# Hybrid attention/RWKV block: the norm behind the mixing reordered, weight roundings moved ahead, and the feed-forward loop's rounding turned by one unit

## The reference

```python
y = rwkv7_scan(rh, heads(decay), kh, vh, kk, ah)
mu = jnp.mean(y, axis=-1, keepdims=True)
var = jnp.mean(jnp.square(y - mu), axis=-1, keepdims=True)
y = ((y - mu) * lax.rsqrt(var + GN_EPS)).reshape(B, T, RW_WIDTH)
y = y * ln_gain.astype(f32) + ln_bias.astype(f32)
bonus = jnp.sum(rh * kh * r_k, axis=-1, keepdims=True) * vh
y = (y + bonus.reshape(B, T, RW_WIDTH)) * g          # o_rw
...
merged = (jax.nn.sigmoid(gate_sb) * (o_sb @ w_branch_sb[l])
          + jax.nn.sigmoid(gate_rw) * (o_rw @ w_branch_rw[l]))
h = h + rms_norm(merged @ w_out[l], norm_mix_post[l])
f = rms_norm(h, norm_ffn_pre[l])
f = (jax.nn.silu(f @ w_ffn_gate[l]) * (f @ w_ffn_up[l])) @ w_ffn_down[l]
h = h + rms_norm(f, norm_ffn_post[l])
```

## Time and profile before

| | us |
|---|---|
| runs (3) | 908.72, 908.95, 911.32; median 908.95 |
| profiled execution, its own time | 913.13 |
| its span, first to last instruction | 911.3 |
| TensorE busy (matmuls) | 878.2 (96% of the span) |
| VectorE / ScalarE / GpSimd busy | 483.1 / 412.6 / 88.8 |
| mean granted TensorE clock | 0.992 of 2.4 GHz |

### The profile page before, as it was taken

One profiled execution on the slowest core, in us unless ns is written; L12 is line 12 of the kernel. 1 busy time (PEld: TensorE's weight loads), 2 busy tenths in 40 slices (PEclk: granted clock), 3 DMA queues, 4 the chain that ended last, 5 costly groups with the idle time before them and its releaser, 6 DMA issues.

```text
span 911.3 us, 19043 instructions
## 1 busy us (share of the span) xinstructions
PE 878.2 (96%) x8257; PEld 728.0 (80%) x8257; DVE 483.1 (53%) x639; ACT 412.6 (45%) x576; POOL 88.8 (10%) x92
## 2 busy tenths in 40 slices
PE   4899999999999999999999999999999999999997
PEld 3899999877777778766787887888888888888886
DVE  5249998437767655636576654444444444422243
ACT  5246555449878765664453542333332222221231
POOL 1014434311010101022200000000000000000000
PEclk9899999999999999999999998999999999999999
DMA  9222322321101121141376413333333333233321
GB/s 286 82 74 67 93 82 81 125 62 38 48 27 38 38 71 39 37 128 50 91 226 203 147 47 93 92 92 92 92 92 92 92 92 93 92 115 93 93 93 69
DMA packets 109150, 83.34 MB, mean 91 GB/s; under 512 B 2910, under 2 KB 99464, under 8 KB 108824
## 3 DMA queue, kind: packets, MB, share of 16 engines
q1 hardware_dynamic: 109080, 82.29, 29.8%
HBM read 76.51 MB, written 5.77 MB: 90 GB/s over the span
## 4 chain that ended last, share of the span: by engine, by line
PE 87%; DVE 7%; ACT 3%; issue 2%; DMA 1%; SPq 0%; POOL 0%; POOLq 0%; DVEq 0%; ACTq 0%
PE psum L566 44%; PE psum L1784 17%; PE psum L1535 9%; PE psum L1572 6%; PE psum L1709 2%; DVE w_lo L556 2%; PE psum L1436 1%; PE psum L1719 1%; PE psum L1827 1%; PE psum L1690 1%; PE psum L1738 1%; DMA w_raw<-in_w_in 1%; DVE shift_diff L1121 1%; ACT w_hi L551 1%; DVE k_mod L1161 1%
## 5 line engine op out<-in xcount | busy, mean ns | idle before, releaser
L566 PE MATMUL psum<-h_hi,w_hi 128*128 128x512 f32 (+1 forms) x736 | 234.2, 354 | 7.5 <-DVE w_lo L556 5.8
L566 PE MATMUL psum<-h_lo,w_hi 128*128 128x512 f32 (+1 forms) x736 | 231.8, 351 | 0.0
L566 PE MATMUL psum<-h_hi,w_lo 128*128 128x512 f32 (+1 forms) x736 | 230.6, 349 | 0.0
L566 PEld LDWEIGHTS psum<-h_hi,w_hi 128*128 128x128 f32 x736 | 129.6, 191 | 30.2 <-DVE w_lo L556 7.0
L556 DVE TENSOR_TENSOR w_lo<-w_raw,w_hi 128x1024 fp32r<-128x1024 f32 x69 | 89.0, 1292 | 119.1 <-ACT w_hi L551 119.1
L566 PEld LDWEIGHTS psum<-h_lo,w_hi 128*128 128x128 f32 x736 | 129.5, 191 | 18.9 <-issue 1.0
L566 PEld LDWEIGHTS psum<-h_hi,w_lo 128*128 128x128 f32 x736 | 129.5, 191 | 18.1
L1382 DVE TENSOR_TENSOR w_lo<-w_raw,w_hi 128x1024 fp32r<-128x1024 f32 x44 | 53.8, 1225 | 135.1 <-ACT w_hi L1052 135.1
L551 ACT ACTIVATE w_hi<-w_raw 128x1024 fp32r<-128x1024 f32 x70 | 73.8, 1056 | 79.5 <-PE psum L1784 63.3
L1052 ACT ACTIVATE w_hi<-w_raw 128x1024 fp32r<-128x1024 f32 x44 | 46.3, 1055 | 69.8 <-PE psum L566 69.8
L1784 PE MATMUL psum<-w_lo,act_hi 128*128 128x512 f32 x144 | 45.7, 389 | 0.0
(11 more groups left out here) (300 smaller groups left out, 1528.2 us busy)
## 6 DMA issues: line engine op xcount, KB each, us to landing
w_raw<-in_w_in SPq DMA_DIRECT2D x42, 512.0 KB, 3.9
w_raw<-in_w_g SPq DMA_DIRECT2D x22, 512.0 KB, 3.9
w_raw<-in_w_u SPq DMA_DIRECT2D x22, 512.0 KB, 3.8
w_raw<-in_w_d SPq DMA_DIRECT2D x22, 512.0 KB, 3.6
w_raw<-in_w_out SPq DMA_DIRECT2D x8, 512.0 KB, 5.8
kept_gates<-gate_raw SPq DMA_DIRECT2D x10, 256.0 KB, 2.7
sig_t<-kept_gates SPq DMA_DIRECT2D x10, 256.0 KB, 3.0
x_in<-in_x SPq DMA_DIRECT2D x4, 512.0 KB, 6.4
```

The lines of the kernel that those rows point to most:

```text
L566: mm = nc.tensor.matmul(o, w[:, (w0 + i) * P:(w0 + i + 1) * P], xs[:, k, c0:c1], start=(n == 0), stop=(n == total - 1))
```

## The change

`gate_up` products of both halves come right behind unit 0, and the bias is added to the bonus once, on GpSimd (`lb`). The norm is then one VectorE instruction that multiplies by gain and reciprocal, and one that adds the bonus; the reciprocal is written over the root, and roots of both halves have their own buffers. ScalarE's gain-and-bias step and GpSimd's bonus addition go. The rounding of the output to `orw_hi`/`orw_lo` (`round`) comes one unit after the multiplication (`out`). Two units of the output projection are split before the last merge (`WO_FIRST = 2`). `ffn_norm(2)` goes ahead of the two `lo_unit`s. In the feed-forward loop ScalarE rounds unit s+3 at step s, after the wait for unit s+1; one rounding stands ahead of the loop.

```diff
+LATE = [("osb", 0), ("lb", 0), ("gates", 0), ("gates", 1), ("square", 0), ("unit", 0), ("var", 0), ("square", 1),
+        ("recip0", 0), ("recip1", 0), ("unit", 1), ("var", 1), ("recip0", 1), ("recip1", 1), ("unit", 2), ("norm", 0),
+        ("out", 0), ("unit", 3), ("round", 0), ("norm", 1), ("out", 1), ("unit", 4), ("round", 1), ("unit", 5)]
-LATE = [("osb", 0), ("square", 0), ("unit", 0), ("var", 0), ("square", 1), ("unit", 1), ("gate", 0), ("unit", 2),
-        ("var", 1), ("out", 0), ("unit", 3), ("gate", 1), ("unit", 4), ("out", 1), ("unit", 5)]
...
+WO_FIRST = 2
...
+                if item == "lb":
+                    pool.wait_ge(bonus_back, 16)
+                    for p in range(PAIRS):
+                        g.tensor_scalar(bonus[:, p, :], bonus[:, p, :], vcol[:, V_LB + p:V_LB + p + 1], None,
+                                        ALU.add).then_inc(post_pool, 1)
...
-                if kind == "gate":
-                    for q in range(2):
-                        p = 2 * i + q
-                        act.wait_ge(post_dve, upto(POST_DVE, "post", i, f"norm{q}"))
-                        s_.activation(y_of(p), y_of(p), ACT.Identity, bias=vcol[:, V_LB + p:V_LB + p + 1],
-                                      scale=vcol[:, V_LG + p:V_LG + p + 1]).then_inc(post_act, 1)
...
                     if what == "branch":
                         hi_unit(act, u + 2)
+                        if u == U_OUT - 1:
+                            for k in range(2, 2 + WO_FIRST):
+                                hi_unit(act, U_OUT + k)
...
+            hi_unit(act, U_FFN + 2)
             with act.Fori(0, N_FFN_LOOP) as i:
                 for s in range(RAW):
                     u0 = U_FFN + s
-                    act.wait_ge(w_used, i * RAW + (u0 + 1))
                     if s % 2 == 0:
                         t = s // 2
+                        act.wait_ge(w_used, i * RAW + (u0 + 1))
                         act.wait_ge(tail_dve, i * (2 * len(TAIL_FFN)) + (FFN_AT + (t - 2) * len(TAIL_FFN) + 1))
                         s_.activation(ffn_t[t][:], bank(2 * t), ACT.Sigmoid).then_inc(f_sig, 1)
-                    v = u0 + 2
+                    v = u0 + 3
+                    act.wait_ge(w_used, i * RAW + (u0 + 2))
                     act.wait_ge(w_in_raw[v % RAW], i * 16 + landed(v))
                     s_.activation(w_hi[v % SPL][:], raw[v % RAW][:], ACT.Copy).then_inc(w_hi_done, 1)
-            for k in range(2, FT):
+            for k in range(3, FT):
                 hi_unit(act, U_DOWN + k)
...
+                if kind in ("recip0", "recip1"):
+                    q = int(kind[5])
+                    dve.wait_ge(post_act, upto(POST_ACT, "post", i, f"root{q}"))
+                    y = yrs[2 * i + q][:]
+                    v_.reciprocal(y, y).then_inc(post_dve, 1)
+                if kind == "norm":
                     for q in range(2):
+                        p = 2 * i + q
+                        dve.wait_ge(post_dve, upto(POST_DVE, "post", i, f"recip{q}"))
+                        v_.scalar_tensor_tensor(y_of(p), y_of(p), vcol[:, V_LG + p:V_LG + p + 1], yrs[p][:],
+                                                ALU.mult, ALU.mult).then_inc(post_dve, 1)
...
+                        v_.tensor_add(y_of(p), y_of(p), bonus[:, p, :]).then_inc(post_dve, 1)
...
                     lo_unit(dve, u + 2)
+                    if u == U_OUT - 1:
+                        for k in range(2, 2 + WO_FIRST):
+                            lo_unit(dve, U_OUT + k)
...
             out_norm(2)
+            ffn_norm(2)
             lo_unit(dve, U_FFN)
             lo_unit(dve, U_FFN + 1)
-            ffn_norm(2)
```

More of the change, by code:

```diff
@@ L111 @@
 BATCHES = [tuple(range(c, min(c + 2, NC_))) for c in range(0, NC_, 2)]
[L114 to L117, removed]
-LATE = [("osb", 0), ("square", 0), ("unit", 0), ("var", 0), ("square", 1), ("unit", 1), ("gate", 0), ("unit", 2),
-        ("var", 1), ("out", 0), ("unit", 3), ("gate", 1), ("unit", 4), ("out", 1), ("unit", 5)]
+POST_ITEMS = {"lb": ([], [], [], ["lb0", "lb1", "lb2", "lb3"]),
+              "gates": (["gate0", "gate1"], [], [], []),
+              "square": ([], ["sq0", "sq1"], [], []),
+              "var": (["var0", "var1"], ["root0", "root1"], [], []),
+              "recip0": ([], [], ["recip0"], []), "recip1": ([], [], ["recip1"], []),
+              "norm": ([], [], ["norm0", "norm1", "add0", "add1"], []),
+              "out": ([], [], ["out0", "out1"], []), "round": ([], ["hi0", "hi1"], [], ["lo0", "lo1"])}
+LATE = [("osb", 0), ("lb", 0), ("gates", 0), ("gates", 1), ("square", 0), ("unit", 0), ("var", 0), ("square", 1),
+        ("recip0", 0), ("recip1", 0), ("unit", 1), ("var", 1), ("recip0", 1), ("recip1", 1), ("unit", 2), ("norm", 0),
+        ("out", 0), ("unit", 3), ("round", 0), ("norm", 1), ("out", 1), ("unit", 4), ("round", 1), ("unit", 5)]
 LATE += [("unit", i) for i in range(2 * AHEAD, len(MERGE) - EARLY)]
@@ L395, in build @@
         ysq = [sb(f"y_sq{i}", [P, SEQ]) for i in range(2)]
-        yrec = [sb(f"y_rec{i}", [P, SEQ]) for i in range(2)]
         yrs = [sb(f"y_rs{i}", [P, SEQ]) for i in range(2)]
         yo = [sb(f"y_o{i}", [P, SEQ]) for i in range(2)]
+        yrs += [sb(f"y_rs{i}", [P, SEQ]) for i in range(2, 4)]
         def at(offset, name, shape, dt=F32):
@@ L742, in _ @@
             for item, r in LATE:
+                if item == "lb":
[3 more added lines that the diff above has]
+                                        ALU.add).then_inc(post_pool, 1)
                 for q in range(2):
                     p = 2 * r + q
[L745 to L750, removed]
+                    if item == "round":
                         pool.wait_ge(post_act, upto(POST_ACT, "post", r, f"hi{q}"))
@@ L956, in _ @@
                         act.wait_ge(post_pe, upto(POST_PE, "post", i, f"var{q}"))
-                        if i:
-                            act.wait_ge(post_dve, upto(POST_DVE, "post", i - 1, f"recip{q}"))
-                        s_.activation(yrs[q][:], bank(6 + q), ACT.Sqrt, bias=small[:, 7:8],
+                        s_.activation(yrs[2 * i + q][:], bank(6 + q), ACT.Sqrt, bias=small[:, 7:8],
                                       scale=1.0 / HD).then_inc(post_act, 1)
-                if kind == "gate":
-                    for q in range(2):
-                        p = 2 * i + q
-                        act.wait_ge(post_dve, upto(POST_DVE, "post", i, f"norm{q}"))
-                        s_.activation(y_of(p), y_of(p), ACT.Identity, bias=vcol[:, V_LB + p:V_LB + p + 1],
-                                      scale=vcol[:, V_LG + p:V_LG + p + 1]).then_inc(post_act, 1)
-                if kind == "out":
+                if kind == "round":
                     for q in range(2):
@@ L987, in _ @@
                         hi_unit(act, u + 2)
-            for k in range(KT - 2):
-                hi_unit(act, U_OUT + k + 2)
+            for k in range(2 + WO_FIRST, KT):
+                hi_unit(act, U_OUT + k)
             def tail_root(block, count):
@@ L1280, in _ @@
             for kind, i in LATE:
-                if kind == "var":
+                if kind in ("recip0", "recip1"):
[4 more added lines that the diff above has]
+                if kind == "norm":
                     for q in range(2):
-                        dve.wait_ge(post_act, upto(POST_ACT, "post", i, f"root{q}"))
-                        v_.reciprocal(yrec[q][:], yrs[q][:]).then_inc(post_dve, 1)
-                if kind == "gate":
+                        p = 2 * i + q
+                        dve.wait_ge(post_dve, upto(POST_DVE, "post", i, f"recip{q}"))
+                        v_.scalar_tensor_tensor(y_of(p), y_of(p), vcol[:, V_LG + p:V_LG + p + 1], yrs[p][:],
+                                                ALU.mult, ALU.mult).then_inc(post_dve, 1)
                     for q in range(2):
-                        y = y_of(2 * i + q)
-                        dve.wait_ge(post_dve, upto(POST_DVE, "post", i, f"recip{q}"))
-                        v_.tensor_mul(y, y, yrec[q][:]).then_inc(post_dve, 1)
+                        p = 2 * i + q
+                        dve.wait_ge(post_dve, upto(POST_DVE, "post", i, f"norm{q}"))
+                        dve.wait_ge(post_pool, upto(POST_POOL, "post", 0, f"lb{p}"))
+                        v_.tensor_add(y_of(p), y_of(p), bonus[:, p, :]).then_inc(post_dve, 1)
                 if kind == "out":
                     for q in range(2):
-                        dve.wait_ge(post_pool, upto(POST_POOL, "post", i, f"bonus{q}"))
+                        dve.wait_ge(post_dve, upto(POST_DVE, "post", i, f"add{q}"))
                         dve.wait_ge(post_pe, upto(POST_PE, "post", i, f"gate{q}"))
@@ L1313, in _ @@
                         v_.tensor_sub(mg_lo[:, j, :], mrg_t[0][:], mg_hi[:, j, :].bitcast(F32)).then_inc(mrg_dve, 1)
-            for k in range(KT - 2):
-                lo_unit(dve, U_OUT + k + 2)
+            for k in range(2 + WO_FIRST, KT):
```

(3 more changed lines are left out.)

## The result

The changed kernel takes 900.15 us, median of 4 runs (899.75 to 901.44); the kernel before, in the same comparison, 909.78. The ratio is 0.9894, 95% interval 0.9880 to 0.9908: 9.6 us less, between 8.4 and 10.9. The forecast was 900.8. Measured a second time on another chip, beside some of the experiments, the ratio was 0.9885 (0.9868 to 0.9902).

A forecast was written before the change was run, and what follows sets the result against it. TensorE was taken to bound the kernel, with 87% of the chain. Closing five idle brackets, 1.72 + 0.82 + 1.87 + 1.97 + 1.79 = 8.17 us, takes 908.95 to 900.8; range 897.4 to 903.4.

The forecast's parts named there:

- The five stalls: TensorE's idle brackets behind the mixing: gate unit 4, first branch unit, output projection, third block, feed-forward loop; gain 8.17 us.
- rival 3: Stalls change places, for example to the last merge or residual's landing, or unprofiled runs have fewer: about 908; chance 0.04.
- the stall at 431.43: Gate unit 4 waits on TensorE for its low part: 1.56 + 0.16 = 1.72 us, foretold to go.
- The bias on GpSimd: Four GpSimd additions beside VectorE's reciprocals behind the mixing: taken as 0 cost, at most 4.8 us if VectorE is shut out.
- rival 2: VectorE late behind the mixing, through the port shared with GpSimd or unit 4's cover of 1.2: 901.8 to 905.6; chance 0.14.
- rival 4: Reciprocal overwriting its input takes double, 6.6 us, in the norm: 10.5 lost, 911.3; chance 0.02.
- The thinnest cover: Behind the mixing, unit 4's low part ends at 423.1, needed by TensorE at 424.31: 1.2 us.
- The rule weighed in the prediction: Two-input VectorE and SBUF-reading GpSimd instructions exclude each other; unit 5's low part could be 1.0 us late.
- The clock: Behind the feed-forward loop's stall the clock fell, costing 2.76 us; the median run was read as free of it.
- the forecast's case: The median run kept its clock, so the change gains the stalls alone: 908.95 - 8.17 = 900.8; chance 0.55.
- rival 1: The median run too had the clock's fall behind the feed-forward stall: 900.8 - 2.8 = 898.0; chance 0.25.
- The profiled execution: The profiled run, with the clock's fall, was to gain 10.9 us: from 913.13 to 902.2, span near 900.4.

The follow-up runs named there:

- a_lodve: The changed kernel with the low parts of the norm's result on VectorE and not on GpSimd: 900.11 us, ratio to before 0.9885.

## Why the prediction was right

- **The five stalls**: foretold 1.72, 0.82, 1.87, 1.97 and 1.79, all gone, and each part alone gave its own, so rival 3 falls. The stretches show 2.76 for 2.54, 1.96 for 1.87, 2.02 for 1.97 and 1.79 for 1.79. The small surplus was left out of the sum: a stream that restarts pays for its first matmul. Behind the stall at 431.43 the next start came 0.35 later, where the cadence is 0.23.
- **The bias on GpSimd**: foretold at 0, bounded by 4.8. The four took 7.04, or 1.76 each, where the nearest row had 2.63, and the first pair of reciprocals, beside them for 3.9 us (403.62 to 407.48), took 6.56, as before. Half of rival 2 falls with that, and the reciprocal in place (rival 4) with the same rows: 6.57 for the second pair. (The 5.9 and 6.8 each at which rival 4 was to turn the verdict come out as 6.0 and 6.7 by its own terms; nothing hung on them.)
- **The thinnest cover**: I gave unit 4, 1.2. It was 1.5 there and 0.8 at unit 6, for which I had worked out 2.2 (433.3 against 435.47); `orw_lo` behind it had 1.1 for 2.8. The step that failed is the 3.9 for `norm` 1 and `out` 1: the multiplications took 2.1 more beside GpSimd's low parts. The rule weighed in the prediction named this kind of collision, and `a_lodve` bears it out: without GpSimd's low parts the same two took 1.41. I had put its effect on unit 5's low part; that one went first, and the multiplications behind it waited. By the Trainium skill (SBUF — State Buffer, "Who interferes with whom") a VectorE instruction with two SBUF inputs is held up beside a GpSimd one that reads SBUF, and one with a single input is not. The trace agrees on both sides: 3.48 for 1.40 with two inputs, 6.56 unchanged for the reciprocals.
- **The clock**: here a reading was wrong, though it moved the result little. I took the runs' two levels (908.7 to 908.9, and 911.3) as one in which the clock did not fall and one in which it did, and the median as free of the fall. In 31 runs of the kernel before 11 lie between 907.97 and 909.25 and 20 between 910.03 and 912.9, but the runs beside the other experiments fall into the gap, and the start up to `osb_hi` spreads by more than the fall costs, so that no single run can be put to one side. The median of the 31 is 910.47, 1.5 over that of the three runs shown. The fall costs 0 to 2.8 behind this stall, 1.8 on average over six profiles, so that the truth lies between the forecast's case and rival 1: 8.17 + 1.8 = 10.0 off, and with restarts a little more, against 9.6 and 10.5 measured. That the after time met the forecast within 0.7 us comes partly from two errors that offset each other: a start 1.5 too low, and 1.5 to 2.3 us of gain left out. That part of the hit is luck.
- **The profiled execution**: foretold 902.2 and a span near 900.4, measured 899.89 and 898.1. Of the 2.3 missing, 2.12 lie ahead of `osb_hi`, where nothing was foretold. The same spread can account for what the sum left open, since this profile's `osb_hi` started latest of all: 913.13 lay 4.2 over the median, and the fall of the clock is 2.8 of that.
- **What was foretold at no cost stayed so**: the last merge 2.5 later, the loads behind it, the loop's later sigmoids. No wait of TensorE names them.

## What to carry to other kernels

Where one engine carries the time, list its idle brackets, price each by the distance of two starts and not by the shown duration, and ask of each part of a change which bracket it closes. On the engines that prepare operands for it, work that the bottleneck needs next goes ahead of work that it needs later; here the norm's new list was worth next to nothing without that order. Once no bracket is left, the covers count: measure each of them, since one partner more (GpSimd beside two-input VectorE work) took 0.9 us from the thinnest without showing in the time.

## What the runs showed of the hardware that was not expected

- The same stall, 1.65 by its bracket, in one and the same kernel, was followed by no loss in one profile and by a loss of 1.7 us to the lower clock in another; over six profiles the loss was 0.1 to 2.8.
- The start of the kernel, up to `osb_hi`, varied by 3.55 us between profiles (391.85 to 395.40), while the stretch behind it repeated within 0.1 in the changed kernel (504.80 and 504.75). Where the clock stays up, two profiles compare a change behind that point more sharply than ten runs do; where it may fall they do not, as the two of one kernel show (506.45 and 508.05).
- Four additions of one number per partition on GpSimd took 7.04 us when the first of them ran beside a VectorE low part (400.18 to 401.41, two inputs), and 6.19, or 1.55 each, in the changed kernel's second profile, where they began behind it. The reciprocals beside them took 6.56 and 6.57, so they were not slowed.
